# Prompt attention two heads at a time, with scaled weights, in a hybrid decoder step on one Trainium2 core

## The reference

```
s = einsum('bqhd,bkhd->bhqk', q, k) * HEAD_DIM ** -0.5
s = s + cq[..., :, None] - ck[..., None, :]        # cumulative log-forget of query and key
p = softmax(where(k_pos <= q_pos, s, -inf), axis=-1)
o = einsum('bhqk,bkhd->bqhd', p, v)
merged = concatenate([rmsnorm(y_ssm, g_ssm_out), rmsnorm(o, g_attn_out)], axis=-1)
out = merged @ w_out
```

## Time and profile before

| | us |
|---|---|
| median of 3 runs | 2384.41 |
| lowest and highest | 2373.78, 2386.98 |
| the profiled execution | 2372.85 |
| its span | 2371.1 |
| prompt attention, first logits to last weighing | 529 to 760 |
| sample attention | 760 to 903 |
| first projection matmuls, norm and transposes of the output | 903 to 923 |
| the rest of the projection | 923 to 1040 |

### The profile page before, as it was taken

One profiled execution on the slowest core, in us unless ns is written; L12 is line 12 of the kernel. 1 busy time (PEld: TensorE's weight loads), 2 busy tenths in 40 slices (PEclk: granted clock), 3 DMA queues, 4 the chain that ended last, 5 costly groups with the idle time before them and its releaser, 6 DMA issues.

```text
span 2371.1 us, 28991 instructions
## 1 busy us (share of the span) xinstructions
PE 2078.4 (88%) x8262; PEld 1117.0 (47%) x8263; DVE 892.5 (38%) x2450; ACT 533.7 (23%) x993; POOL 300.3 (13%) x236
## 2 busy tenths in 40 slices
PE   4797899998888888978978999899899999998990
PEld 1456555446666334545434444444445455544450
DVE  2827400315554222234423333333333333333338
ACT  3423221015544112033111111111111111111122
POOL 0010100000000030000001122122122222221124
PEclk7898889999998998988988999999899999999995
DMA  9531200022000443001148899899888778898843
GB/s 335 218 155 23 113 0 1 0 76 58 18 1 18 131 138 133 0 19 58 52 176 279 288 298 293 277 295 297 265 273 250 250 241 259 266 288 281 287 102 137
DMA packets 100878, 394.20 MB, mean 166 GB/s; under 512 B 27279, under 2 KB 30003, under 8 KB 71996
## 3 DMA queue, kind: packets, MB, share of 16 engines
q1 hardware_dynamic: 70020, 302.44, 34.4%
q0 software_dynamic: 24768, 90.19, 15.9%
q10 hardware_dynamic: 6024, 0.73, 0.2%
HBM read 329.16 MB, written 62.57 MB: 165 GB/s over the span
## 4 chain that ended last, share of the span: by engine, by line
PE 27%; DMA 22%; issue 5%; SPq 4%; DVE 2%; ACT 1%; POOL 0%; POOLq 0%; DVEq 0%; ACTq 0%
DMA arena<-in_w_exp_down 22%; PE psum L961 11%; PE psum L989 5%; PE psum L830 5%; SPq L2209 2%; PE psum L947 1%; SPq L2204 1%; SPq L2205 1%; DVE arena L1607 1%; PE psum L858 1%; PE psum L864 1%; DVE arena L1617 1%; PE psum L871 0%; PE psum L809 0%; PE psum L854 0%
## 5 line engine op out<-in xcount | busy, mean ns | idle before, releaser
L961 PE MATMUL psum<-arena 128*128 x1360 | 631.1, 619 | 55.2 <-SPq L2230 51.5
L961 PEld LDWEIGHTS psum<-arena 128*128 128x128 f32 x1360 | 261.1, 197 | 358.3 <-issue 358.3
L989 PE MATMUL psum<-arena,tail 128*128 x672 | 302.3, 592 | 0.0
L2057 POOL DMA_INDIRECT moe_rows<-arena x84 | 133.4, 1588 | 815.2 <-ACT arena L1941 291.4
L1563 DVE TENSOR_TENSOR arena<-arena,psum 128x256 f32<-128x256 f32 x85 | 35.8, 421 | 499.2 <-ACT arena L1927 499.2
L989 PEld LDWEIGHTS psum<-arena,tail 128*128 128x128 f32 x672 | 121.1, 190 | 120.5 <-issue 120.5
L1927 ACT ACTIVATE arena<-psum 128x256 f32<-128x256 f32 x85 | 32.7, 385 | 644.3 <-PE psum L961 644.3
L678 PE MATMUL psum<-arena 128*128 128x512 f32 (+1 forms) x384 | 126.5, 493 | 0.0
L830 PE MATMUL psum<-arena 128*128 128x512 f32 (+1 forms) x288 | 124.3, 593 | 0.9 <-ACT arena L1853 0.5
L1541 DVE TENSOR_TENSOR arena<-tail,arena 128x1152 bf16<-128x1152 f32 x89 | 119.6, 1344 | 0.0
L1941 ACT ACTIVATE arena<-psum,arena 128x512 f32<-128x512 f32 x84 | 57.7, 687 | 213.3 <-PE psum L989 213.3
(11 more groups left out here) (486 smaller groups left out, 2342.1 us busy)
## 6 DMA issues: line engine op xcount, KB each, us to landing
arena<-in_w_exp_gate SPq DMA_DIRECT2D x64, 1024.0 KB, 5.3
arena<-in_w_exp_up SPq DMA_DIRECT2D x64, 1024.0 KB, 9.4
arena<-in_w_exp_down SPq DMA_DIRECT2D x64, 1024.0 KB, 12.3
arena<-in_w_ada SPq DMA_DIRECT2D x24, 1024.0 KB, 7.6
arena<-in_w_ada_final SPq DMA_DIRECT2D x8, 1024.0 KB, 6.5
arena<-in_cache_k SPq DMA_DIRECT2D x32, 256.0 KB, 3.4
arena<-in_cache_v SPq DMA_DIRECT2D x32, 256.0 KB, 2.9
arena<-in_w_in SPq DMA_DIRECT2D x1, 6176.0 KB, 18.5
```

The costliest lines, as they stand in the source:

```text
L961: ins = pe.matmul(slot[2 + par].rearrange("p (h n) -> p h n", h=2), xTs[:, par, k, :], ring_gu[:, at, :, k, :].rearrange("p a h n -> p (a ...
L989: ins = pe.matmul(slot[1][:, n * 512:(n + 1) * 512], hTs[:, k, :], ring_d[:, at, k, n, :].rearrange("p a n -> p (a n)"), start=(k == 0), s ...
L2057: pool.indirect_dma_start(y_dram, bass.IndirectOffsetOnAxis(ap=s_idx[:, par:par + 1], axis=0), y_buf[:, par, :], None, compute_op=ALU.add) ...
```

## The change

Heads are taken in pairs. 32 steps run over four pairs of heads, query tiles i = 7 down to 0 (PAIRS).
- qT holds two heads to 128 rows without zeros; the logits of both heads are matmuls with 64 rows each, to slots 0 and 1, alternating.
- GpSimd adds the causal mask to the diagonal block of neg_c ahead of each step (mask), which VectorE did on the logits.
- The weights are scaled by the reciprocal of their sum before the transposes: the even head's by GpSimd (normalise), the odd head's by VectorE (one_over_sum). The exponential is written in place.
- Weighing takes the values as the stationary side (64 columns) and 128 moving columns; both heads go to one slot, on partitions 0 to 63 and 64 to 127. The output comes out transposed, and ScalarE copies it straight to oT.
- The spreading matmuls of the next pair of heads (L717 now, half a head at a time) go to slots 4 and 5.
- The squares of the prompt's rows are summed by GpSimd (14 operations) and by eight small matmuls among the samples; the scale by the inverse root moves behind the projection, into VectorE's addition of the halves. Only the samples' rows are still transposed.
- The shared expert's weights start to load when the projection is done. The zeroing of qT goes.

```diff
-        qT = arena(21536, H, T)
+        qT = arena(21536, KA, T)
-        sc = arena(8192, 2, SEQ)
-        pr = arena(10240, 2, SEQ)
-        pt = arena(12288, 2, SEQ)
-        o_tok = arena(14336, NT, DA)
+        sc = arena(8192, 4, SEQ)
+        pt = arena(25888, 4, SEQ)
+        oT = arena(14336, KA, T)
...
-        ATT = [(i, h) for h in range(H) for i in range(8)]
+        PAIRS = [(i, j) for j in range(KA) for i in range(7, -1, -1)]
...
+        SPREAD_AT = (6, 5, 4, 3)
...
+            def logits(p):
+                i, j = PAIRS[p]
+                for a in range(2):
+                    fill(pe, ("L", 2 * p + a), a)
                 for c0 in range(0, (i + 1) * P, 512):
                     c1 = min(c0 + 512, (i + 1) * P)
+                    for a in range(2):
+                        h0, h1 = a * DH, (a + 1) * DH
+                        ins = pe.matmul(slot[a][:, c0:c1], qT[h0:h1, j, i * P:(i + 1) * P], kT[h0:h1, j, c0:c1], start=True, stop=True)
...
+            def turn_weights(p, a):
+                i, j = PAIRS[p]
+                it = 2 * p + a
+                pe.wait_ge((pn_ready, w1_scaled)[a], p + 1)
+                for q0 in pt_keys(p):
+                    b = 2 + (q0 // 4)
+                    fill(pe, ("PT", it, q0), b)
+                    for m in range(q0, min(q0 + 4, i + 1)):
+                        ins = pe.transpose(slot[b][:, (m - q0) * P:(m - q0 + 1) * P], sc[:, it % 4, m * P:(m + 1) * P], ident)
                     full(ins, ("PT", it, q0))
...
+                        ins = pe.matmul(slot[4 + p % 2][a * DH:(a + 1) * DH, 0:P], v[:, m, (2 * j + a) * DH:(2 * j + a + 1) * DH],
+                                        pt[:, (2 * p + a) % 4, m * P:(m + 1) * P], start=(m == 0), stop=(m == i), skip_group_check=True)
...
+            logits(0)
+            for p in range(len(PAIRS)):
+                if p + 1 < len(PAIRS):
+                    logits(p + 1)
+                turn_weights(p, 0)
+                if p:
+                    weigh(p - 1)
+                turn_weights(p, 1)
+                if spread_of(p):
+                    spread_sums(*spread_of(p), 4 + (p + 1) % 2)
+            weigh(len(PAIRS) - 1)
...
+                ins = dve.reciprocal(att_one[:, 8 + it % 4:9 + it % 4], att_one[:, 4 + it % 4:5 + it % 4])
+                if it % 2 == 0:
+                    ins.then_inc(recip_ready, 1)
+                    return
+                dlink(ins)
+                n = (PAIRS[it // 2][0] + 1) * P
+                ts(sc[:, it % 4, 0:n], sc[:, it % 4, 0:n], att_one[:, 8 + it % 4:9 + it % 4], None, ALU.mult).then_inc(w1_scaled, 1)
...
+            for p in range(len(PAIRS) + 1):
+                for a in range(2):
+                    if p < len(PAIRS):
+                        exponentials(2 * p + a)
+                    if p:
+                        weights_out(2 * p - 2 + a)
+                if p >= 2:
+                    attention_out(p - 2)
+                if p and spread_of(p - 1):
+                    spread_out(*spread_of(p - 1))
...
+            def normalise(it):
+                n = (PAIRS[it // 2][0] + 1) * P
+                pool.wait_ge(recip_ready, it // 2 + 1)
+                pool.tensor_scalar(sc[:, it % 4, 0:n], sc[:, it % 4, 0:n], att_one[:, 8 + it % 4:9 + it % 4], None, ALU.mult).then_inc(pn_ready, 1)
+
+            for p in range(len(PAIRS) + 1):
+                if p < len(PAIRS):
+                    mask(p)
+                if p:
+                    normalise(2 * p - 2)
...
-                ins = tt(mix, mix, slot[1][0:m, :], ALU.add)
+                ins = stt(mix, slot[1][0:m, :], rstd[0:m, t:t + 1], mix, ALU.mult, ALU.add)
```

More of the change, by code:

```diff
@@ L702, in _, with spread_sums @@
             full(ins, "LF")
-            def spread_sums(h, s_):
-                fill(pe, ("CB", h), s_)
-                for n in range(2):
-                    ins = pe.matmul(slot[s_][:, n * 512:(n + 1) * 512], ident[0:H, h:h + 1].to_broadcast([H, P]), c_row[:, n * 512:(n + 1) * 512], start=True, stop=True)
-                full(ins, ("CB", h))
-            spread_sums(0, 0)
+            def spread_sums(h, n, s_):
+                fill(pe, ("CB", h, n), s_)
+                full(pe.matmul(slot[s_], ident[0:H, h:h + 1].to_broadcast([H, P]), c_row[:, n * 512:(n + 1) * 512], start=True, stop=True), ("CB", h, n))
@@ L712, in _ @@
+            for i in range(4):
+                spread_sums(i // 2, i % 2, 4 + i % 2)
             slots.wait_empty(pe, ("V", 7))
-            def logits(it):
-                i, h = ATT[it]
-                fill(pe, ("L", it), it % 2)
+            def logits(p):
+                i, j = PAIRS[p]
+                for a in range(2):
+                    fill(pe, ("L", 2 * p + a), a)
                 for c0 in range(0, (i + 1) * P, 512):
                     c1 = min(c0 + 512, (i + 1) * P)
-                    ins = pe.matmul(slot[it % 2][:, c0:c1], qT[:, h, i * P:(i + 1) * P], kT[:, h // 2, c0:c1], start=True, stop=True)
-                full(ins, ("L", it))
@@ L722, in weigh @@
[L722 to L739 removed]
+                    for a in range(2):
+                        h0, h1 = a * DH, (a + 1) * DH
+                        ins = pe.matmul(slot[a][:, c0:c1], qT[h0:h1, j, i * P:(i + 1) * P], kT[h0:h1, j, c0:c1], start=True, stop=True)
+                        if c1 == (i + 1) * P:
+                            full(ins, ("L", 2 * p + a))
@@ L796, in _ @@
                     add_rows(b - 1)
+                if b == 4:
+                    pe.wait_ge(o_squares, 1)
+                    fill(pe, "OSS", 4)
+                    for t in range(8):
+                        ins = pe.matmul(slot[4][:, t:t + 1], o_acc.rearrange("p (c t) -> p t c", t=CH)[:, t], ones_col, start=True, stop=True)
+                    full(ins, "OSS")
                 if b + 1 < NSEQ:
@@ L833, in _ @@
             project_out(0, 0)
[L835 to L842 removed]
+            slots.wait_empty(pe, "SR")
+            fill(pe, "OT", 2)
+            for k in range(KA):
+                ins = pe.transpose(slot[2][:, k * P:k * P + NS], o_smp[:, k * P:(k + 1) * P], ident[0:NS, 0:NS])
+            full(ins, "OT")
             for t in range(NT):
```

227 lines of the change are left out of this document (107 added, 120 removed).

## The result

The changed kernel takes 2439.99 us (median of 4 runs, 2434.28 to 2447.17), the kernel before took 2379.59 beside it (4 runs, 2373.78 to 2386.98). The ratio is 1.0254, 95% interval 1.0205 to 1.0302: slower by 60 us. The profiled execution took 2435.26 us, its span 2433.5 us.

The account below looks back on a forecast made before the run. A loop of waits closed once per pair was taken to bound attention: between 255 and 313 us, middle 284, 53 more than now; less 13 elsewhere gives +40 on 2372.85, so 2412 us, range 2352 to 2448.

Parts of the forecast that it names:

- The wait that takes its place: Attention: instruction order closes a loop through the engines once per pair of heads, 49.8 us a sweep without a port conflict.
- rival 1: TensorE's clock stays at half through the whole attention stage: 313 us there, 2442 us in all; chance 0.17.
- VectorE against GpSimd: Attention: VectorE's odd-head scaling waits for the rest of GpSimd's scaling at a shared port, 7.3 us a sweep; lower bound nothing.
- The clock: Attention: TensorE's granted clock falls towards half; 255 us at full and 313 at half, middle 284 taken.
- rival 2: No port conflict and full clock: attention 230 us, as long as before, so the kernel is faster at 2359 us; chance 0.17.
- way A: Attention's longest chain per pair, through VectorE's additions, reciprocals and odd scaling, then exponential, transposes and logits: 48.6 us a sweep.
- way B: Attention's other chain per pair, through GpSimd's scaling, both heads' transposes, weighing and logits: 1.1+1.10k us for k key tiles.
- Spreading the sums: Attention: twelve spreading matmuls wait for ScalarE's output copy and delay the next logits, 28.6 us; longer start 2.5 more.
- TensorE's side by side tiles: Attention: 64-row and 64-column matmuls of two heads run side by side, logits 0.21k us per pair for k key tiles.
- Rival 4: 64-wide tiles don't run side by side, so logits and weighing double: attention 295 us, 2424 in all; chance 0.12.
- rival 3: The loop doesn't bind and engines run at their throughput: attention 146 us, 2275 in all; chance 0.06.
- The rest: Outside attention: norm before the projection 12.5 us less, copy links 1 less, column sums 0.5 more, squares hidden; together -13.

## Why the prediction was right on the sign and short on the size

**The wait that takes its place: right.** It named the loop, its members and their order, and taking a member out of it at any of three places took 35 to 116 us off the stage. The measured 2439.99 us lies inside the stated range of 2352 to 2448, but 28 above the forecast and outside the forecast's own 2385 to 2435. It falls on rival 1's 2442, whose condition, half clock through the whole stage, did not hold: 40 of 198 us of TensorE's work lie at 0.95 or more. That the number fits is luck.

**VectorE against GpSimd: this step failed.** The full wait, 7.3 us a sweep or 29 in all, was put on the odd scaling beside GpSimd's scaling. In the changed kernel the odd scaling takes 753 ns at 1024 columns in the middle of GpSimd's 2846: no wait. Odd scalings of 0.5 to 0.8 us were among the prediction's own signs of being wrong. The earlier trace rows showed the conflict for a GpSimd tensor_tensor, and a GpSimd scaling has one tensor input; the added experiment with two inputs shows the wait just as it was assumed. The prediction's bound "nothing" was the true end. In its sum that takes off 25 us, not 29, because without the wait the way through GpSimd is the longer at k of 6 to 8.
The Trainium skill (SBUF — State Buffer, "SBUF: two separate sides") has the lock between a VectorE instruction in a two-port mode and any GpSimd instruction. The two-input case agrees with it; the one-input case does not show it, and there the measurement decides. That VectorE's scaling runs in such a mode no run shows directly; it takes 753 ns where the additions of the same width take 1275.

**The clock: the step that was mis-sized.** The middle between full and half was taken, +29 us. Without the port's wait the prediction's full-clock sum is its rival 2's 230 us, of which 2.5 are the longer start and lie ahead of the first logits. The stage took 307.7, 80 more than the 227.5 that are left. The experiment with the gap filled bounds the clock's part: the stage fell by 54 us with 76 us of added work in it, and TensorE's own work by 61. So the clock cost some 54 to 61 us, a few more against a clock of 1.00, and about twice the 29 put down. The other 20 to 26 are a full-clock sum that was too short; at which member of it stays open.
The reason given for the middle, that the rows show both levels, holds: 133 and 40 of 198 us. What was wrong is the distance between the bounds. The 255 was way A with the port's wait and the 313 way B, which hardly needs the port (1.1+1.74k, or 71.4 us a sweep), so the wait that wasn't there hid a part of what the clock costs way B. From 230 to 313 the middle is +41. The 22 us for spreads in the 313 have no working behind them either; 28.6 and 0.87 for each of twelve would be 39. That it was way B is what the experiments show, since a shorter GpSimd instruction shortened the stage by 24 us and none at all by 15.
In attention the errors had opposite signs, -25 for the port and +51 for the clock and the short sum. With +2 at the start, +1 from the round figure for the stage before and -7 in the rest they leave the profiled execution 22 us above the 2412.85, and the median lies 5 above that execution.

**Spreading the sums: about right.** 28.6 us at full clock; moving them gained 35, a better clock included. Spreads that wait for ScalarE are in the table of waits, twelve times. The longer start was put at 2.5 us and took 4.8.

**TensorE's side by side tiles: right.** Logits of both heads took 3.36 us for 896 columns at a granted 0.50 (618.81), or 0.96 per 512 columns at full clock, near the 0.9 that was asked for; one head after the other would be 1.7. Rival 4 falls, and rival 3 with the waits above. For the changes between tile sizes, which were priced at 26 us and left out, TensorE's records show nothing: over the stage its matmuls stand idle for 0.0 us ahead of the weighing and for 2.7 ahead of the logits, and VectorE ended those. Ends are modelled, so a small cost could hide there.

**The rest: -13 predicted, -20 found (the start not counted), by other terms.** The norm is as worked out: 12.8 against 12.5, and the projection goes on behind the new sums of squares without a gap. "GpSimd's squares lie beside the sample stage" failed: the first matmul on the queries came 13.4 us behind the last weighing (855.05) instead of 8.2 (+5.2), with VectorE's instructions stretched beside GpSimd's; moving the squares gave 3.1 of it back. The column sums cost eight times the 0.5 us put down:

```profile
928.17 3.97 PE L822 MATMUL psum<-tail,arena 128*128 128x1 f32 x16
```

Each moves one column, but each also loads 128x128 weights, 0.25 us a record at a granted 0.71. Another 4 us are the weighing of the past, before and then here:

```profile
L809 PE MATMUL psum<-arena 128*64 128x512 f32 x64 | 36.5, 724 | 5.7 <-ACT arena L1836 5.7
L836 PE MATMUL psum<-arena 128*64 128x512 f32 x64 | 40.5, 794 | 5.7 <-ACT arena L1868 5.7
```

And 1.7 are the key transposes, at a stage clock of 0.85 instead of 0.91. That makes 15 us, where 14 were found.
Behind the projection 21 us went away that the prediction did not have: 7 up to the first expert, 14 in the experts, whose code is the same. The eleven other traces of the changed form show 1312 to 1323 us there, against 1309.5 in this one. The kernel before has one trace (1331), and its runs spread from 2352 to 2389, so whether this belongs to the change stays open.

## What to carry to other kernels

When work moves from one engine to several in a chain, add up one round through the chain in the order in which the instructions are queued, and ask of each engine what it could do two rounds ahead: here one line in TensorE's order was worth 116 us, and choices between the engines changed sign once it was made. Waits can cost clock as well as time: here TensorE worked for 64% of the stage in bursts at a mean of 0.63, and filling its gap gave back 54 us. So read the granted clock in the windows in which the engine works. When two bounds of a sum are taken, check that both go by the same way; these didn't, and the term between them came out at half its size. What rows show of a conflict holds for the forms of instruction seen in them, not for the pair of engines.

## What the runs showed of the hardware

- A GpSimd tensor_scalar on a float32 SBUF tile took 2.85 us at 1024 columns and left a VectorE tensor_scalar of the same width beside it alone (753 ns); a GpSimd tensor_tensor of the same tile with a broadcast operand took 1.89 us and made it wait (1369 ns).
- Beside GpSimd's squares eight 64x64 copies of VectorE took 4.91 us, without them 1.61.
- 76 us of matmuls that nobody reads shortened a stage from 307.7 to 253.5 us, with the granted clock going from 0.68 to 0.94 and the time of the other matmuls from 198.2 to 137.0 us.
- A matmul that moves one column past 128x128 float32 weights took 0.25 us a record in a row of 16 (3.97 us), at a granted clock of 0.71.
